# A two-layer decoder step on one core: second layer's loads earlier, its scores in fp32, and both tails reordered

## The reference

```
layer 0 (even): proj = x @ w_in;  A: RWKV-7 scan with a 64x64 state for each of 8 heads
                                  B: S5, 32 groups of 16 channels, 64 complex states, then GELU and GLU
layer 1 (odd):  proj = x @ w_in;  C: stick-breaking attention, 8 heads of 64
                                  D: gated linear attention, 4 heads (keys 64, values 128)
out = concat(branch_1 * silu(gate_1), branch_2 * silu(gate_2)) @ w_out
x   = LayerNorm(alpha * x + out)          after each layer
```

```
z        = q @ k.T * d**-0.5 + bias                       # for each head
log_1mb  = where(key < query, log_sigmoid(-z), 0)
att      = where(key < query, exp(log_sigmoid(z) + sum of log_1mb over later keys), 0)
out      = att @ v
```

## Time and profile before

| | us |
|---|---|
| median of 3 runs | 3307.34 (3305.88 to 3318.5) |
| profiled execution, its own time | 3314.94 |
| its span | 3313.2 |
| TensorE busy | 2906.6 |
| VectorE busy | 2179.1 |
| ScalarE busy | 1262.2 |
| GpSimd busy | 826.0 |
| mean granted clock of TensorE | 0.95 |

### The profile page before, as it was taken

One profiled execution on the slowest core, in us unless ns is written; L12 is line 12 of the kernel. 1 busy time (PEld: TensorE's weight loads), 2 busy tenths in 40 slices (PEclk: granted clock), 3 DMA queues, 4 the chain that ended last, 5 costly groups with the idle time before them and its releaser, 6 DMA issues. The chain is left out here.

```text
span 3313.2 us, 70723 instructions
## 1 busy us (share of the span) xinstructions
PE 2906.6 (88%) x27987; PEld 2407.6 (73%) x27987; DVE 2179.1 (66%) x3338; ACT 1262.2 (38%) x2272; POOL 826.0 (25%) x726
## 2 busy tenths in 40 slices
PE   8799999977898958898799999979868988978698
PEld 7699999966776746676697877857646666658476
DVE  9526666547676637985358777613449899876587
ACT  1015555434444443342011011111128888864332
POOL 4100000012222322110211111112126676654221
PEclk9899999989999988998899999979989999999799
DMA  5524554464444555653559999963521101025542
GB/s 179 199 88 146 149 159 150 135 164 105 108 109 93 133 148 153 184 158 93 199 176 313 339 352 334 311 205 126 167 97 52 65 17 50 14 50 173 185 148 89
DMA packets 470755, 506.43 MB, mean 153 GB/s; under 512 B 200018, under 2 KB 363075, under 8 KB 465035
## 3 DMA queue, kind: packets, MB, share of 16 engines
q1 hardware_dynamic: 373466, 341.17, 34.1%
q10 hardware_dynamic: 88000, 143.93, 12.5%
q0 software_dynamic: 8960, 16.81, 1.8%
HBM read 360.68 MB, written 141.31 MB: 152 GB/s over the span
## 5 line engine op out<-in xcount | busy, mean ns | idle before, releaser
L2754 POOL TENSOR_TENSOR sp_att<-sp_beta,sp_left 128x512 f32<-128x512 f32 (+3 forms) x320 | 318.0, 1003 | 195.8 <-DVE sp_left L2710 184.1
L102 PE MATMUL po_acc<-po_x_high,po_w_low 128*128 128x412 f32 (+1 forms) x840 | 306.8, 365 | 36.9 <-POOL po_w_low L95 18.1
L102 PE MATMUL pe_acc<-pe_x_high,pe_w_low 128*128 128x412 f32 (+1 forms) x840 | 304.9, 363 | 22.4 <-DVE pe_x_low L95 14.8
L103 PE MATMUL po_acc<-po_x_low,po_w_high 128*128 128x412 f32 (+1 forms) x840 | 299.0, 356 | 0.0
L104 PE MATMUL po_acc<-po_x_high,po_w_high 128*128 128x412 f32 (+1 forms) x840 | 298.8, 356 | 0.0
L104 PE MATMUL pe_acc<-pe_x_high,pe_w_high 128*128 128x412 f32 (+1 forms) x840 | 295.7, 352 | 0.0
L103 PE MATMUL pe_acc<-pe_x_low,pe_w_high 128*128 128x412 f32 (+1 forms) x840 | 295.5, 352 | 0.0
L2710 DVE TENSOR_TENSOR_SCAN sp_left<-sp_z,sp_left,sp_zero 128x512 f32<-128x512 f32 x192 | 235.3, 1266 | 14.4 <-ACT sp_z L2654 12.6
L2441 DVE TENSOR_TENSOR po_work<-po_work,po_q 128x1024 f32<-128x1024 f32 x128 | 175.9, 1374 | 84.0 <-DMA po_work<-in_cache_k 78.3
L102 PEld LDWEIGHTS po_acc<-po_x_high,po_w_low 128*128 128x128 f32 x840 | 162.6, 194 | 85.2 <-ACT po_o L1183 31.5
L2646 ACT ACTIVATE sp_beta<-sp_z,sp_bias 128x512 f32<-128x512 f32 (+3 forms) x320 | 183.6, 631 | 72.7 <-PE sp_z L2585 44.8
(11 more groups left out here) (489 smaller groups left out, 7219.6 us busy)
## 6 DMA issues: line engine op xcount, KB each, us to landing
po_work<-in_cache_k SPq DMA_DIRECT2D x256, 256.0 KB, 5.1
po_work<-in_cache_v ACTq DMA_DIRECT2D x256, 256.0 KB, 4.7
scratch_ops<-pe_work SPq DMA_DIRECT2D x160, 128.0 KB, 2.1
out_z<-pe_o SPq DMA_DIRECT2D x84, 206.0 KB, 2.7
out_z<-po_o ACTq DMA_DIRECT2D x84, 206.0 KB, 4.6
pe_w<-in_w_e SPq DMA_DIRECT2D x21, 512.0 KB
po_w<-in_w_o ACTq DMA_DIRECT2D x21, 512.0 KB
rc_opx<-scratch_ops SPq DMA_DIRECT2D x16, 640.0 KB, 5.5
```

The lines of the kernel that those rows point to most:

```text
L102: pe.matmul(out, ll, rh, start=start, stop=False)
L103: pe.matmul(out, lh, rl, start=False, stop=False)
L2754: pool.tensor_tensor(att[h][:, n % 3, 0:w], be[h][:, n % 4, 0:w], left[h][tile(n) % 2][:, at + 1:at + 1 + w], ALU.mult).then_inc(at_ok[h], 1)
```

## The change

1. **rc.** POOL's store of the S5 table moves from behind the chunk phases to ahead of them in each step. The first chunk's operands are loaded in two parts.
2. **Even tail.** The block loads come before the output weights on SP; on ACT and DVE all eight weight splits come after the first block's gates and sigmoids. In a block's loads yb and gate_b come first. `EvenSamples` does the drive of S5 with 8 transposes and 4 fp32 matmuls on TensorE; its big state operations come in nine pieces, two in each iteration and none before the loop; the small work has one piece for b = 1 to 5 behind the eviction of tile 2b+1, first half.
3. **Odd tail.** TensorE: `back(1)` before tile 1 instead of behind it. ACT: squares and back of block 0 before the weight casts, and block 1 before the first norm. DVE: `scaled(1)` between the first two evictions.
4. **Both tails.** The norm is two scalar_tensor_tensor operations.
5. **po.** ACT requests the weights of group 1 at its start, and those of group i+2 at the first slot of group i.
6. **pv.** Keys and queries of all columns are resident and loaded in column blocks; the low-rank columns are loaded once, 16 rows; the alpha matmul contracts over 16 rows.
7. **sp.** Scores are one fp32 matmul for each head from q and k as loaded, in two buffers each; the splits on DVE are gone; the first loads are in parts with semaphores of their own; the gates' sigmoid has a buffer, and `collect` waits for half gates.

Cut to its core:

```diff
 # rc, POOL
+    def gpsimd_first(self, pool, t):
+        i = t - self.LT - 1
+        if 0 <= i < HG:
+            pool.wait_ge(self.tb_ev, i + 1)
+            pool.dma_start(self.trans[:, i], self.bi[i % 2][:, :, :]).then_inc(self.bi_st[i % 2], 16)
...
             for t in range(STEPS):
+                s5.gpsimd_first(pool, t)
                 for c, ph in running(t):
                     phase(c, ph)
                 s5.gpsimd(pool, t)
 # Tail, SP
-        for k in range(4):
-            weights(k)
+        if not self.even:
+            for k in range(4):
+                weights(k)
         for dst, src in maps:
             sp.dma_start(dst, src).then_inc(self.cst_b, 16)
         load_rest(0)
-        for k in range(4, KT):
+        for k in range(0 if self.even else 4, KT):
             weights(k)
 # Tail, TensorE
-        tile(1, (0,))
-        centre(1)
-        glu(1)
-        tile(1, (1,))
-        back(1)
-        turned(0)
+        if self.even:
...
+        else:
+            back(1)
+            tile(1)
...
-                if b >= self.es.DRIVE:
+                if b in self.es.UNITS:
                     pe.wait_ge(self.yT_ok, 2 * b)
 # Tail, ACT
-        weights(0)
         squares(0)
-        for k in range(1, 4):
-            weights(k)
         back(0)
-        gates(0)
+        if not self.even:
+            for k in range(3):
+                weights(k)
         act.wait_ge(self.cst_b, self.CST_B)
+        gates(0)
         sigmoids(0)
-        for k in range(4, KT):
+        for k in range(0 if self.even else 3, KT):
             weights(k)
 # Tail, DVE
-            link(dve.tensor_scalar(y, y, self.mv[h][r, 0:1], self.sd[h][r, 1:2], ALU.subtract, ALU.mult))
-            link(dve.tensor_tensor(y, y, self.g[r, :], ALU.mult))
-            dve.tensor_tensor(y, y, self.b[r, :], ALU.add).then_inc(self.y_ok, 1)
+            link(dve.scalar_tensor_tensor(out=y, in0=y, scalar=self.mv[h][r, 0:1], in1=self.g[r, :], op0=ALU.subtract,
+                                          op1=ALU.mult))
+            dve.scalar_tensor_tensor(out=y, in0=y, scalar=self.sd[h][r, 1:2], in1=self.b[r, :], op0=ALU.mult,
+                                     op1=ALU.add).then_inc(self.y_ok, 1)
...
             evict(t + 1, 0)
-            next(samples, None)
+            if self.even:
+                self.es.vector(dve, b)
 # EvenSamples, TensorE and DVE, b = 2
+            for k in range(4):
+                mm = pe.matmul(self.tr[:, 0, k * 64:(k + 1) * 64], self.lT[:, k, :],
+                               self.ud[:, k, :, :].rearrange("p g b -> p (g b)"), start=True, stop=True)
+            dve.wait_ge(self.bu_pe, 1)
+            dve.tensor_tensor(self.hn, tr[:, 0, 0:NS * G].rearrange("p (g b) -> p b g", b=NS), self.w, ALU.add).then_inc(self.new, 1)
 # po, ACT
+            pj.load_w(act, 1)
             act.wait_ge(tab, 16)
...
-                    if t in pj.opens and i + 1 < len(ODD_GROUPS):
-                        pj.load_w(act, i + 1)
+                    if t in pj.opens and i + 2 < len(ODD_GROUPS):
+                        pj.load_w(act, i + 2)
 # sp, TensorE
-                for t, (lhs, rhs) in enumerate(((ql, kh), (qh, kl), (qh, kh))):
-                    for h in (0, 1):
-                        r = slice(64 * h, 64 * h + 64)
-                        mm[h] = pe.matmul(zb[h][b][:, 0:w], lhs[q][r, cq].bitcast(F32R), rhs[q][r, ck].bitcast(F32R),
-                                          start=(t == 0), stop=(t == 2 and not diagonal(n)))
+                for h in (0, 1):
+                    r = slice(64 * h, 64 * h + 64)
+                    mm[h] = pe.matmul(zb[h][b][:, 0:w], qt[q][r, cq], kt[q][r, ck], start=True, stop=not diagonal(n))
 # sp, DVE
-                at = n % PER - (PER - 22)
-                if 0 <= at < 8 and n // PER + 1 < PAIRS:
-                    splits(n // PER + 1, at)
 # pv
-        qk, ad = two("qk", [P, 2, GW]), two("ad", [P, GW])
+        qk, ad = s.sb("qk", [P, 4, COLS]), s.sb("ad", [R_G, COLS])
-                pe.matmul(gb[q][:, 0:w], wt[:, q * P:(q + 1) * P], ad[q][:, 0:w], start=True, stop=True).then_inc(a_pe, 1)
+                pe.matmul(gb[q][:, 0:w], wt[0:R_G, q * P:(q + 1) * P], ad[:, columns(n // 2)], start=True, stop=True
+                          ).then_inc(a_pe, 1)
```

More of the change, by code:

```diff
@@ L785, in gpsimd @@
         weights(0)
-        weights(2)
-        weights(4)
+        if not self.even:
+            weights(2)
         low(0)
-        weights(6)
+        for k in ((2, 4, 6) if self.even else (4, 6)):
+            weights(k)
         for t in range(1, TT + 1):
@@ L848, in norm @@
             h, r = t % 2, slice(0, self.rows(t))
-            if t % 2 or t == 0:
+            if t % 2 or (t == 0 and self.even):
                 act.preload_act_table_set(LN_EXP)
@@ L872, in scalar @@
         act.wait_ge(self.eset, 2)
-        weights(0)
         squares(0)
-        for k in range(1, 4):
-            weights(k)
-        back(0)
-        gates(0)
-        act.wait_ge(self.cst_b, self.CST_B)
-        sigmoids(0)
-        for k in range(4, KT):
-            weights(k)
-        norm(0)
-        front(1)
-        put(0)
-        back(1)
-        put_turned(0)
+        back(0)
+        if not self.even:
+            for k in range(3):
+                weights(k)
+        act.wait_ge(self.cst_b, self.CST_B)
+        gates(0)
+        sigmoids(0)
+        for k in range(0 if self.even else 3, KT):
+            weights(k)
+        if self.even:
+            norm(0)
+            front(1)
+            put(0)
+            back(1)
+            put_turned(0)
+        else:
+            front(1)
+            back(1)
+            norm(0)
+            put(0)
         for b in range(1, self.NB):
@@ L1028, in vector @@
             unit(0)
+        else:
+            weights(1)
         gated(0)
         high(0)
-        weights(5)
-        weights(7)
+        for k in ((1, 3, 5, 7) if self.even else (3, 5, 7)):
+            weights(k)
         high(1)
         evict(0, 0)
-        evict(0, 1)
-        spread(0)
         if self.even:
+            evict(0, 1)
+            spread(0)
             centre(1, 0)
             centre(1, 1)
-        norm(0)
-        evict(1, 0)
-        if self.even:
+            norm(0)
+            evict(1, 0)
             unit(1)
-        scaled(1)
-        high(2)
-        next(samples, None)
+            scaled(1)
+            high(2)
+        else:
+            scaled(1)
+            evict(0, 1)
+            spread(0)
+            high(2)
+            norm(0)
+            evict(1, 0)
         for b in range(1, self.NB):
```

312 lines of the change are left out of this document (165 added, 147 removed).

## The result

The changed kernel takes 3230.11 us (median of 4 runs, 3223.7 to 3236.72), the kernel before 3308.03 (4 runs). The ratio is 0.9758, 95% interval 0.9729 to 0.9788. The forecast was 3225, range 3203 to 3266. In a later series (e13) the changed kernel came to 0.9756 (0.9733 to 0.9779) of the kernel before, on the same chip.

What follows compares the result with a forecast made beforehand. TensorE, busy 2907 of 3313 us, was taken as the bound, so time could come only from its idle 406 us or shorter work. Stage terms -4 -20 -20 -11 -15 -12 = -82 took the median 3307.34 to 3225, range 3203 to 3266.

Steps and rivals of the forecast that it cites:

- the store's flight: RWKV stage: POOL's store leaves sooner, but its flight stays as the next late thing; -4 taken, bounds 0 and -9.5.
- stays above 350: Even tail: the prediction counts as wrong if this stage stays above 350 us.
- the 3.3 for the clock: Even tail: low clock after long gaps goes, -2.3 for the gap of 10.1 and -1 for that of 7.0.
- VectorE no longer has two weight splits in: Even tail: the 11.5 wait for cat_low shortens by 1.5 because its chain loses two weight splits on VectorE.
- rival C: Both tails give little, TensorE waiting for VectorE and late weight split; half of -32 lost, 3241; chance 0.15.
- late next: Odd projection: with weights loaded early, POOL's split of 1.04 + 2.34 is the next late thing; +1.5 left.
- the fp32 scores: Attention: one fp32 matmul per head replacing three fp32r passes costs +8, bounds 0 and +29.
- 0.43 apart: Attention: sign expected in the profile after, fp32 score records 0.43 apart with x2 in a stretch.
- rival B: Attention: TensorE is the step's only limit and the whole 29 for fp32 scores shows; 3246; chance 0.17.
- The line and the price: Odd tail: block 1's sums before tile 1 remove the second cat_low wait, -8.1, and -2.6 for the clock.
- A: Attention: both heads' fp32 score matmuls run one after the other, 116 more, 3341, so slower; chance 0.03.
- D: Odd projection: early weight loads only move the gap to a page wait, the -20 is lost, 3245; chance 0.08.

Runs made afterwards that it cites:

- e13: The changed kernel itself, without a further edit, measured again in a later series on the same chip; 3231.63 us, ratio 0.9756.
- e11: Changed kernel with POOL's store order, the three-operation norm and the old values stage restored; rc 538.6, values 227.9, odd tail 240.7, even tail 350.3 us.
- e1: Changed kernel with the even tail's block 1 loads issued behind the first four output weights instead of all eight; ratio 0.9771, tail 346.2 us.
- e5: Kernel before with one edit, the odd projection's weights requested two groups ahead; ratio 0.9933, stage 627.9 instead of 647.8 us.
- e2: Changed kernel with attention scores as three fp32r passes over constant operands, without splits; attention 495.8 us.
- e7: Changed kernel with the odd tail's sums of block 1 put behind tile 1 again on TensorE; stage 248.7 us.
- e3: Changed kernel with both heads' score matmuls on the same 64 rows of the array; 3326 us, attention 616.6 us.

## Why the prediction was right

The total came 5 above the forecast. By stages, the two profiled spans, and the means over all profiles with the old and with the new code of a stage (profiles with another edit in that stage are left out; po has one profile of the old code):

```
                        rc     oe     po     pv     sp     oo
forecast              -4    -20    -20    -11    -15    -12
before to changed     -7.9  -16.4  -20.3  -14.4  -12.3   -9.7
difference of means  -14.8  -12.3  -23.0  -14.6  -12.6   -8.6
```

The stages that were not touched give -1.9 between the two spans. Every part went the way that was said, but the terms miss by up to 4 (up to 11 in the means), too small in rc, po and pv and too large in oe, sp and oo. That these misses cancel to a few microseconds is luck.

- **RWKV stage, too small.** L1710's wait fell by 7.8 and not by 4: the store's flight, which the prediction left in place, was hidden once the store was issued ahead of the phases. e11 shows the wait by itself. Over all runs the stage differs by more than that, 540.6 in the mean of three against 525.8 in that of ten. Of these 14.8 TensorE's idle time has 8.5 (78.9 to 70.4), which is the wait and up to 2 at the first operand load (10.5 to 8.6, from two pieces). The other 6.3 is the same matmuls taking longer at a lower granted clock (0.94 in two of the three, 0.94 to 0.97 in the ten); whether the edit or chance set that clock stays open.
- **Even tail, too large, and for partly wrong reasons.** The drive and the two early sample operations went as said: 10.1 and 9.6 of waits became 1.9 in all. The forecast of 20 came out as 16.4, and as 12.3 in the means, and the sign "stays above 350" was crossed in three profiles of the same code (350.3, 350.8, 351.3) and not in the others. Two steps failed. The start gained 3.4 of 5, and of the 3.3 for the clock nothing can be read over the runs: TensorE's busy time is 302 and 307 with the old code and 304 to 309 with the new. "VectorE no longer has two weight splits in" the chain to cat_low was wrong: the wait is 11.5 in both, since those splits had run ahead of the sigmoids before. And I had the late weight split cost +1 in the first product, but not what stands behind it in SyncE's queue: block 1's loads, a new wait of 7.4. The queue that a step is moved past was followed only as far as the first product. e1 shows that this wait was worth 2 to 4, since VectorE's lag lies right behind it.
- **The Trainium skill's rule on the shared interface** (GPSIMD Engine Reference, section 1) had one consequence here, rival C. e11 bounds it: with the three-operation norm back, the even tail's waits at those two places grow by 1.4 and TensorE's idle time does not, so the form of the norm decides little either way there. The page also names instructions in a 2-port perf mode beside those with two inputs; whether the one-input L1013 is one is not shown, so its 2.91 neither supports nor contradicts the rule.
- **Odd projection, right**, by e5 alone 19.9 and by the kernel's change 20.3. Of these, 16.6 are the waits for po_w_low and 4.5 TensorE's busy time (583.6 to 579.1), where -5 was said for the clock. What the part called "late next", POOL's split beside a slot, is the 1.5 that was left.
- **Values stage, too small.** 10.1 of waits went, as said; the bound was -14 and the stage gave -14.4. Waits for x_low fell from 3.3 to 1.1 as well, which I had left out; by e11 they come back (3.4) with the old loads. The rest, 2.4, is less busy time of TensorE (201.4 to 199.0). Which of the two changes to the loads brought it is not separated.
- **Attention.** The start gave -7.5 as worked out (first wait 20.7 to 13.2). The fourth pair, which had no splits, became 3.6 longer, and the second and third 1.1 shorter, so the splits gave 4.7 for each, as said. The first pair became 6.4 shorter, 5.3 more than the next two, where 2.5 was said for its gates; its first 28 us stand at a granted clock of 0.62 before and 0.70 after, so a part of that can be the clock's. The term that was mis-sized is that of the fp32 scores: 8 expected, 12.3 measured (e2), and 3.6 for the fourth pair alone, that is 14 for four. I set a block's 0.85 of columns beside 1.00. But the 0.85 leaves out the 0.2 that comes on top, and the 1.00 was an untypical block. The usual one of the kernel before takes 0.90:

```profile
2829.89 0.50 PE L2585 MATMUL sp_z<-sp_k_high,sp_q_low 64*128 64x512 f32 x2
...
2830.79 1.09 PE L2600 MATMUL sp_t<-sp_id,sp_att 128*128 128x128 f32 x8
```

So fp32 is dearer by 0.16 a block, and the sign "0.43 apart" failed: the two records of a score matmul start 0.53 apart. The 29 of rival B does not show either: three fp32r passes have such an extra too (0.90 against 0.64), so TensorE's busy time grew by 18.8 and not by 29, and a third of that fell into its idle time. The stage came to 508 where about 505 was said.

- **Odd tail.** The line and the price were right (11.3 in e7 against 10.7). The start was not: the first sums came 2.2 earlier, but cat_low waited 14.2 instead of 12.7, so 1.5 of it was given back. The norm had 0.8 in the sum and is worth about 3 by e11. The line's 11.3 and these 3 are more than the stage's 9.7; what costs the difference of about 5 (the other new orders, or an overlap of the two) is open.

Of the rivals, A's condition is shown false, and its price of 116 was measured as 108.5: 86 at the full clock, since idle time took up the rest, and 22 at a lower one, so the agreement with 116 is luck. B and C are each true in part (B by 4 of its 21; of C's 16, 6 between the two profiles and 11 in the means); D fell.

## What to carry to other kernels

When a load is moved behind others in a queue, count what now stands behind those others' waits: a ring of buffers that blocks the queue delays everything that is issued after it. A wait that goes is worth its length only if nothing else is late right behind it; the 7.4 here was worth 2 to 4, as VectorE's lag lay behind it. And work can move to an engine that sits in the chain of each step, if it comes in pieces shorter than its idle time there: what cost 4.6 a pair on VectorE cost about 2 in the whole stage on POOL, in pieces of 0.6 and 1.27.

## What the hardware showed that I had not expected

A block of score matmuls on 64 rows, standing between blocks on all 128 rows, takes 0.20 to 0.26 more than its columns: 1.06 for 0.85 and 0.63 for 0.43 (two fp32 records of 512 and of 256 columns, both heads at once), 1.91 for 1.71 (four in a row, e3), 0.90 for 0.64 (three fp32r passes, e2 and the kernel before). In e3's trace it is the first and the last record that have the longer spacing, 0.54 and 0.52 against 0.43. The Trainium skill (TensorEngine Tiling, Key Properties) says that a change of the tiling mode drains the engine; an extra once for each block and independent of its length agrees with that, though no run here varied the mode by itself, and a cost of the weight loads at a block's two ends is not excluded.
